# Layer 0 of a streaming encoder step: prompt rows turned as loaded, first loads and first projections in another order

## What is computed

```
h  = rms_norm(x, ln_attn[l])                      # x * 1/sqrt(mean(x*x) + eps) * gain
z  = einsum('btd,de->bte', h, w_in[l])            # 1024 -> 1184 columns
#    columns 0:512 q_a, 512:640 k_a, 640:768 v_a, 768:1024 q latent, 1024:1152 kv latent, 1152:1184 rotary key
#    every part: rms_norm per head, rotary turn of q_a, k_a and the rotary key
o  = concat(sliding-window attention (keys: band or cache), latent attention (keys: own or cached latent))
x  = x + einsum('btm,md->btd', o, w_o[l])
x  = x + (swiglu(rms_norm(x)) if l == 0 else top-2-of-8 experts(rms_norm(x)))
```

## Time and profile before

| | |
|---|---|
| runs | 1201.98, 1202.36, 1204.39 us; median 1202.36 |
| the profiled execution's own time | 1203.37 us |
| its span in the trace | 1201.5 us |
| attention of layer 0 | 0 to 146 us |
| dense layer | 146 to about 380 us |
| attention of layer 1 | to about 500 us |
| experts | about 505 to 1190 us |

### The profile page before, as it was taken

One profiled execution on the slowest core, in us unless ns is written; L12 is line 12 of the kernel. 1 busy time (PEld: TensorE's weight loads), 2 busy tenths in 40 slices (PEclk: granted clock), 3 DMA queues, 4 the chain that ended last, 5 costly groups with the idle time before them and its releaser, 6 DMA issues.

```text
span 1201.5 us, 24345 instructions
## 1 busy us (share of the span) xinstructions
PE 1179.6 (98%) x10285; PEld 618.4 (51%) x10285; DVE 548.7 (46%) x1035; ACT 329.9 (27%) x612; POOL 80.3 (7%) x179
## 2 busy tenths in 40 slices
PE   8999999999999999999999999999999999999998
PEld 5566699999995566533333333333333333333254
DVE  2677534544414667533433434354264244334334
ACT  2576533443324556310210210210200200211101
POOL 4132000000001120000000000000000100100100
PEclk9999999999999999999999999999999999999999
DMA  9261294554530353999999999999999999999996
GB/s 304 60 168 37 92 285 150 174 175 132 162 125 1 63 132 125 352 369 375 406 389 413 398 399 413 399 398 414 399 396 415 399 399 415 390 408 414 392 410 256
DMA packets 114104, 348.56 MB, mean 290 GB/s; under 512 B 8592, under 2 KB 34032, under 8 KB 103808
## 3 DMA queue, kind: packets, MB, share of 16 engines
q1 hardware_dynamic: 108656, 335.55, 74.4%
q0 software_dynamic: 3648, 10.60, 3.1%
q10 hardware_dynamic: 1744, 1.61, 0.4%
HBM read 339.70 MB, written 8.04 MB: 289 GB/s over the span
## 4 chain that ended last, share of the span: by engine, by line
PE 86%; DMA 6%; DVE 4%; ACT 2%; SPq 1%; issue 1%; DVEq 0%; ACTq 0%
PE ps L2439 34%; PE ps L2446 17%; PE ps L2344 12%; PE ps L2075 8%; PE ps L2360 6%; DMA ring<-in_moe_w_gate 2%; DMA ring<-in_moe_w_down 2%; DMA ring<-in_w_in 2%; SPq L736 1%; PE ps L2274 1%; PE ps L2221 1%; PE ps L2236 1%; PE ps L2166 1%; PE ps L2155 1%; PE ps L2088 1%
## 5 line engine op out<-in xcount | busy, mean ns | idle before, releaser
L2439 PE MATMUL ps<-ring,xg 128*32 128x512 f32 (+1 forms) x1792 | 197.6, 547 | 1.2 <-DMA ring<-in_moe_w_gate 0.8
L1857 DVE STREAM_TRANSPOSE am<-act_m 32x256 f32<-32x256 f32 (+1 forms) x288 | 172.6, 599 | 4.7
L2439 PE MATMUL ps<-ring_more,xg 128*32 128x512 f32 (+1 forms) x1280 | 149.7, 571 | 0.0
L1351 DVE TENSOR_TENSOR w_lo<-ring,w_hi 128x2048 fp32r<-128x2048 f32 (+1 forms) x34 | 76.0, 2234 | 96.2 <-ACT w_hi L941 96.2
L2075 PE MATMUL ps<-ring,hT 128*128 128x512 f32 x256 | 115.4, 596 | 0.1
L2439 PEld LDWEIGHTS ps<-ring,xg 128*32 128x32 f32 x1792 | 58.0, 110 | 111.2 <-issue 106.4
L1842 DVE TENSOR_TENSOR act_m<-act_m,ps 64x512 f32<-64x512 f32 (+1 forms) x24 | 15.2, 635 | 213.1 <-ACT act_m L1290 213.1
L2439 PE MATMUL ps<-ring_more,am 128*32 128x512 f32 x896 | 108.9, 592 | 0.0
L2446 PE MATMUL ps<-ring,xg 128*32 128x512 f32 (+1 forms) x896 | 106.7, 547 | 0.0
L2344 PE MATMUL ps<-hT_hi,w_hi 128*128 128x288 f32 x352 | 104.3, 296 | 0.5 <-DVE hT_lo L1725 0.5
L2344 PE MATMUL ps<-hT_lo,w_hi 128*128 128x288 f32 x352 | 103.8, 295 | 0.0
(11 more groups left out here) (388 smaller groups left out, 1539.2 us busy)
## 6 DMA issues: line engine op xcount, KB each, us to landing
ring_more<-in_moe_w_down SPq DMA_DIRECT2D x64, 1024.0 KB, 16.0
ring<-in_moe_w_gate SPq DMA_DIRECT2D x48, 1024.0 KB, 17.0
ring_more<-in_moe_w_up SPq DMA_DIRECT2D x48, 1024.0 KB, 16.2
ring<-in_moe_w_gate SPq DMA_DIRECT2D x32, 768.0 KB, 18.6
ring_more<-in_moe_w_gate SPq DMA_DIRECT2D x16, 1024.0 KB, 14.7
ring<-in_moe_w_up SPq DMA_DIRECT2D x16, 1024.0 KB, 18.4
ring<-in_moe_w_down SPq DMA_DIRECT2D x16, 1024.0 KB, 15.5
ring<-in_moe_w_up SPq DMA_DIRECT2D x16, 768.0 KB, 14.7
```

Source lines behind the costliest of these rows:

```text
L1351: V.tensor_tensor(lo[:, 0:size], src[:, 0:size], hi[:, 0:size].bitcast(F32), ALU.subtract).then_inc(lo_ready, 1)
L1857: ins = V.transpose(am[GRAN * q:GRAN * q + GRAN, c % 2, 0:nk, GRAN * g:GRAN * g + GRAN], src)
L2439: ins = mm_(ps[GRAN * s_:GRAN * s_ + GRAN, b, 0:half], x[:, GRAN * g:GRAN * g + GRAN], w[:, half * h:half * h + half], start=(n == 0), sto ...
```

## The change

Prompt tiles of layer 0 are turned as they were loaded, without the scaling on VectorE, and their scale is applied when the projections are taken out, as in layer 1. TensorE turns tile 0 first, then the gains' rows, the decode tile, and tile 1 only after the first half block of tile 0. The decode projection comes behind three half blocks of tile 0 instead of two, and `za` 0,1,1 and `za` 1,0,1 are each one step of their kind earlier. Of seven filler matmuls in front of the `h` steps two stay. SyncE loads prompt tile 1 ahead of the third quarter of the weights, and the constants ahead of the fourth. GpSimd loads the router and layer 1's caches after the last row step of layer 0, and the caches have a semaphore for each layer.

```diff
-PE_ORDER = [[("h", 2), ("h", 0), ("h", 1), ("za", 0, 0, 0), ("za", 0, 0, 1), ("tc",), ("za", 2), ("zc", 0), ("za", 0, 1, 0),
-             ("item", 0), ("za", 1, 0, 0), ("tq", 2), ("za", 0, 1, 1), ("titem", 0), ("item", 1), ("s", 0), ("item", 2),
-             ("za", 1, 0, 1), ("za", 1, 1, 0), ("p", 0), ("za", 1, 1, 1), ("titem", 1), ("o", 0), ("tq", 0), ("zc", 1),
+PE_ORDER = [[("h", 0), ("ln",), ("h", 2), ("za", 0, 0, 0), ("h", 1), ("za", 0, 0, 1), ("za", 0, 1, 0), ("tc",), ("za", 2), ("zc", 0),
+             ("item", 0), ("za", 0, 1, 1), ("za", 1, 0, 0), ("tq", 2), ("za", 1, 0, 1), ("titem", 0), ("item", 1), ("s", 0), ("item", 2),
+             ("za", 1, 1, 0), ("p", 0), ("za", 1, 1, 1), ("titem", 1), ("o", 0), ("tq", 0), ("zc", 1),
...
-              ("isq", 0), ("ir", 0), ("tqe", 2), ("zev", 0, 1), ("tie", 0), ("isq", 1), ("zr", 0), ("e", 0), ("ir", 1),
+              ("isq", 0), ("ir", 0), ("zev", 0, 1), ("tqe", 2), ("tie", 0), ("isq", 1), ("zr", 0), ("e", 0), ("ir", 1),
...
-DVE_ORDER = [[("x1", 2), ("ln",), ("x1", 0), ("hd", 2), ("x1", 1), ("hd", 0), ("hd", 1), ("z1", 2), ("z2", 2), ("i1", 0),
+DVE_ORDER = [[("x1", 2), ("ln",), ("r1", 0), ("hd", 0), ("hd", 2), ("r1", 1), ("hd", 1), ("z1", 2), ("z2", 2), ("i1", 0),
...
-WAITING = [{("h", 2): 4, ("h", 0): 2, ("h", 1): 1, ("p", 1): 1, ("o", 1): 4, ("s", 3): 1, ("p", 2): 3, ("o", 2): 2, ("hf", 1): 6},
+WAITING = [{("h", 2): 2, ("p", 1): 1, ("o", 1): 4, ("s", 3): 1, ("p", 2): 3, ("o", 2): 2, ("hf", 1): 6},
...
-            for t in TILES:
+            def load_rows(t):
+
                 src = a["x_sample"][0] if t == 2 else a["x_prompt"][0, t * P:(t + 1) * P, :]
                 sp.dma_start(xres[0:ROWS[t], t, :], src).then_inc(loaded_x[t], 16)
+
+            load_rows(2)
+            load_rows(0)
...
                 if key == ("in", 0, 1, 0):
+                    load_rows(1)
+                elif key == ("in", 0, 1, 1):
                     sp.dma_start(cst[:, P:CONST_W], consts[:, P:CONST_W]).then_inc(loaded_c, 16)
...
-            pool.dma_start(wr[:, :, :], a["moe_router"][0].rearrange("(k p) e -> p k e", p=P)).then_inc(loaded_cache, 16)
-            for l in range(DEPTH):
+            def load_caches(l):
...
+            load_caches(0)
...
                 pool.wait_ge(rows_ready, 3 * l + 3)
+                if l == 0:
+                    pool.dma_start(wr[:, :, :], a["moe_router"][0].rearrange("(k p) e -> p k e", p=P)).then_inc(loaded_router, 16)
+                    load_caches(1)
...
-                        by = 1.0 if l == 0 else rsx[:, t:t + 1]
-                        if l:
-                            act.wait_ge(scale_x, t + 1)
+                        by = rsx[:, t:t + 1]
+                        act.wait_ge(scale_x, 2 * l + t + 1)
...
-            pe.wait_ge(loaded_ln, 32)
             ident = C("ident")
-            tr(ps[:, 0, 0:4 * KD], ln_rows[0:4 * KD, :], ident[0:4 * KD, 0:4 * KD]).then_inc(ln_done, 1)
...
+                    if kind == "ln":
+
+                        pe.wait_ge(loaded_ln, 32)
+                        tr(ps[:, 0, 0:4 * KD], ln_rows[0:4 * KD, :], ident[0:4 * KD, 0:4 * KD]).then_inc(ln_done, 1)
...
-                    elif kind == "h" and l == 1 and which[0] < 2:
+                    elif kind == "h" and which[0] < 2:
...
-                        wait_out(pe, ("tz", KD - 3))
+                        if l:
+                            wait_out(pe, ("tz", KD - 3))
+                        else:
+                            pe.wait_ge(loaded_x[t], 16)
...
-                        pe.wait_ge(loaded_cache, CACHES_IN)
+                        pe.wait_ge(loaded_cache[l], CACHES_IN)
```

More of the change, by code:

```diff
@@ L426, in build @@
         loaded_g = [sem(f"loaded_g{l}") for l in range(DEPTH)]
-        loaded_cache = sem("loaded_cache")
+        loaded_cache = [sem(f"loaded_cache{l}") for l in range(DEPTH)]
+        loaded_router = sem("loaded_router")
         loaded_col = sem("loaded_col")
@@ L659, in build @@
         GAINS_IN = 16 * len(GAIN)
-        CACHES_IN = 16 * (1 + 4 * DEPTH)
+        CACHES_IN = 16 * 4
         block = ctx.enter_context(nc.Block())
@@ L776, in _ @@
         def _(pool):
-            pool.dma_start(wr[:, :, :], a["moe_router"][0].rearrange("(k p) e -> p k e", p=P)).then_inc(loaded_cache, 16)
-            for l in range(DEPTH):
-                pool.dma_start(kc[:, l, :], a["cache_swa_k"][l, 0].rearrange("s h d -> s (h d)")).then_inc(loaded_cache, 16)
-                pool.dma_start(vc[:, l, :], a["cache_swa_v"][l, 0].rearrange("s h d -> s (h d)")).then_inc(loaded_cache, 16)
-                pool.dma_start(ckvc[:, l, :], a["cache_mla_ckv"][l, 0]).then_inc(loaded_cache, 16)
-                pool.dma_start(krc[:, l, :], a["cache_mla_krope"][l, 0]).then_inc(loaded_cache, 16)
+            def load_caches(l):
+                pool.dma_start(kc[:, l, :], a["cache_swa_k"][l, 0].rearrange("s h d -> s (h d)")).then_inc(loaded_cache[l], 16)
+                pool.dma_start(vc[:, l, :], a["cache_swa_v"][l, 0].rearrange("s h d -> s (h d)")).then_inc(loaded_cache[l], 16)
+                pool.dma_start(ckvc[:, l, :], a["cache_mla_ckv"][l, 0]).then_inc(loaded_cache[l], 16)
+                pool.dma_start(krc[:, l, :], a["cache_mla_krope"][l, 0]).then_inc(loaded_cache[l], 16)
+            load_caches(0)
             for l in range(DEPTH):
@@ L841, in rope_part @@
                     if t == 2:
-                        pool.wait_ge(loaded_cache, CACHES_IN)
+                        pool.wait_ge(loaded_cache[l], CACHES_IN)
                     own = krc[:, l, :] if t == 2 else kr[0:r, min(t, 2), :]
@@ L1437, in expert_tables @@
                 dve.wait_ge(tables_clear, 1)
+                dve.wait_ge(loaded_router, 16)
                 V.tensor_tensor(wr[:, :, :], wr[:, :, :], bc(ln_cols[:, 3 * KD:4 * KD], NE), ALU.mult).then_inc(router_scaled, 1)
@@ L1975, in _ @@
                         busy(ps[:, 0, :], WAITING[l][step])
-                    if kind == "hf" and l == 1:
+                    if kind == "ln":
+                        pe.wait_ge(loaded_ln, 32)
+                        tr(ps[:, 0, 0:4 * KD], ln_rows[0:4 * KD, :], ident[0:4 * KD, 0:4 * KD]).then_inc(ln_done, 1)
+                    elif kind == "hf" and l == 1:
                         t, = which
@@ L2003, in _ @@
                         busy(pair(key), WAITING[l].get(step, 0))
-                        wait_out(pe, ("tz", KD - 3))
+                        if l:
+                            wait_out(pe, ("tz", KD - 3))
+                        else:
+                            pe.wait_ge(loaded_x[t], 16)
                         for k in range(KD):
-                            if k == 4:
+                            if l and k == 4:
                                 wait_out(pe, ("tz", KD - 1))
```

## The result

The changed kernel takes 1208.09 us (median of 7 runs, 1206.34 to 1209.52); the kernel before, run beside it, 1203.06 (7 runs, 1201.98 to 1204.41). The ratio is 1.0037, 95% interval 1.0028 to 1.0046. So it is slower, by 3.4 to 5.5 us with that interval; the forecast was 1199.4 with a range up to 1202.2.

The account below looks back on a forecast made before the run. TensorE was taken as the bound, with the first weights' transfers on the chain early. Terms -3.43 moved block, +0.13 later start, 0 tables, +0.3 behind made -3.0: 1202.36 to 1199.4 us, range 1197.5 to 1202.2.

Parts of the forecast that it names:

- One projection step moves into the wait: Layer 0 prelude: `za` 0,1,0 runs before the fourth weight quarter lands, taking 3.43 us out of what follows.
- Less ahead in the queues: Prelude loads: with 240 KB fewer and a new order, first quarter at 9.9, tile 1's rows 14.4, fourth quarter 25.8.
- Is TensorE in time?: Prelude: three blocks done by 24.4, no wait for the fourth quarter, `zc` 0 ends at 31.5; gain 3.3 us.
- rival 3: `za` 0,0,0 to `za` 0,1,0: clock stays low, each block costs 3.43 us more; +5, 1207 us; chance 0.07.
- Tables: GpSimd's tables after the gain loads: gains land at 29.2, tables end at 34.3, just out of the way; cost 0.
- Rival 1: Gains land at 31 or later, TensorE stands at `tq` 2 for 1 to 2.5 us: 1201.2; chance 0.25.
- What comes after 34.80 is released by events of the kernel ... so what is won by then is won at the end: After the prelude: time won by 34.80 reaches the end of the kernel unless a wait eats it.
- the rest of the attention: Layer 0 attention behind the prelude: slower evacuations, VectorE timing and fewer blocks before `p` 0 cost 0.3 us together.
- Rival 2: Layer 0 attention: ScalarE and VectorE set its end, gain becomes waits before `titem` 1 and 2; 1202 to 1202.6; chance 0.08.
- Five of seven filler matmuls go; by themselves they cover nothing: Prelude, before the `h` steps: removing five fillers was given no cost of its own in the sum.
- dense layer and experts as long as before: Everything behind layer 0's attention: durations unchanged, listed as a sign that the forecast was right.
- The rule I weighed: Prelude: dropped fillers and a stand at tile 1's rows risk the lower clock; by it alone, some us worse.

Follow-up runs that it names:

- the second profile of the changed kernel: The changed kernel, unaltered, run once more beside later versions: 1207.66 us, ratio 1.0036.
- item 1 early: `i2` 1 ahead of tile 0's `z2` on VectorE, item 1's root earlier on ScalarE: changed kernel with five fillers back 1200.48 us; kernel before 1203.47.
- the kernel with the order alone: Kernel before with item 1 early and `za` 0,1,0 ahead of the cached keys' turning and decode projection, loads as before: 1206.74 us.
- the fillers late: Changed kernel with five filler matmuls added in layer 1's attention (`o` of group 2) instead of the prelude: 1205.79 us, ratio 1.0023.
- the fastest version with three fewer: Changed kernel with five fillers back, item 1 early and keys' up-projection loaded before queries', then three prelude fillers taken out: 1204.13 us.

## Why the prediction was wrong

*One projection step moves into the wait* was right: TensorE reached the end of `zc` 0 at 31.0 (31.5 forecast).

*Less ahead in the queues* was right but for one transfer: first quarter 9.9 (9.9; the exact hit is luck, three more profiles with the same prelude have 10.1 to 10.7), tile 1's rows 14.0 (14.4). I named `b_w_ukv` among the loads and gave it no landing time. It came at 31.9, and `item` 0 waited 0.95 us (0.47 in the second profile of the changed kernel).

*Is TensorE in time?* was right: three blocks done at 24.1 (24.4), eight records on the lower level in 6.55 us, full clock from 16.3. So rival 3 (clock stays low) fell.

*Tables*: gains landed at 27.0 (29.2) and the tables ended at 32.8 (34.3), 1.6 us before `z2` took them; `z2` was released by ScalarE's root. Rival 1 fell.

*"What comes after 34.80 is released by events of the kernel ... so what is won by then is won at the end"* failed, with its term of 0.3 for *the rest of the attention*. `item` 0 was 2.7 us early, and at `p` 0 TensorE stood 2.96 us. My own text had the reason: "Between `s` 0 and `p` 0 stands one block now instead of two". I weighed that against the decode exponentials only, which end "with little room", and didn't look for what else `p` 0 waits on: the pair that `i2` 1 empties, 8 us behind the start of `s` 0 in both kernels, and half a microsecond ahead of `p` 0 in the kernel before. With a block less in that stretch TensorE has 5.2 us of work for those 8. "TensorE arrives 3 us earlier at items 1 and 2" was wrong too: `item` 1 starts at 45.79, before at 44.99, since a third half block now stands in front of it. Rival 2 was this in kind (chance 0.08); it named other places (`titem` 1 and 2) and I argued it away by the hand-over at 64.76, which shows who is last there and not who waits earlier. The runs show it: with item 1 early 3.2 us come back in the changed order, and in the kernel before nothing does.

*"Five of seven filler matmuls go; by themselves they cover nothing"* and *dense layer and experts as long as before* failed. They cover nothing indeed, but they are length. The loss, 3.16 us of standing and 1.7 us at the lower clock less 1.3 us of waits that went, is most of the difference between 1208 and 1203, and no rival held it. The rows before show no stand, so I couldn't have known the sign; that the program's length changes in front of a loop's exit I could have listed as a cost bounded by nothing.

The rule I weighed, that idle stretches send the clock back, would have been of use at another place than I looked. The trace agrees behind the loop: 3.16 us without work, then 0.50. Ahead of `p` 0 it doesn't: 2.96 us without work, then 1.00 in the same kernel.

On code, the Trainium skill, "Runtime: NRT & Kernel Launch" (Instruction fetch mechanics), says that instructions come in blocks of 16 KiB, prefetched strictly in sequence, and that a taken branch to outside what is held costs a fetch. The block size agrees with the profile page of the changed kernel (0.67 MB in 41 packets, 16 KB each; the page of the kernel before has the same line):

```profile
q8 instruction: 41, 0.67, 0.2%
```

The stand seen here is not at a branch taken but behind the exit of a loop, where the next block in sequence is asked for only at the exit (its packet starts 1.4 to 1.7 us later); it lasts 2.3 to 3.8 us by where the cut lies.

## What to carry to other kernels

Before crediting a gain on one engine, find the next place where it meets another engine's chain and measure the room there; moving work of the bound engine out of a wait wins only what the other chains can follow. Work moved from behind a step to in front of it delays what the step starts and leaves less to cover it: count both. When instructions are added to or taken from the busiest engine of a program with a hardware loop, look first at the instructions right behind the loop's exit in the new profile: an idle time released by "issue" there can be code arriving late, which the packets of the instruction queue in the loop's first turn show, and a few harmless instructions anywhere in front move it away. Filler instructions have three effects to be told apart (cover a wait, hold the clock, shift the code), and it takes one run each: drop them, and put them elsewhere.

## What was unexpected in the hardware

- Leaving a loop can cost a fetch: the code behind a fixed cut arrives 4.0 to 4.2 us after the exit, in six profiles of five kernels. Eight records more in front of the cut shortened the stand by 0.86 us by arithmetic and 0.86 (3.16 to 2.30) by measurement.
- A loop of some 600 us was held whole: its code packets came in its first turn, and between 600 and 1100 us none of the fourteen profiles has one.
- Idle time of TensorE of about the same length was followed by the lower clock level at one place and mostly not at another. Behind the loop 2.3 to 3.8 us of it were, in five profiles of six; the price was 1.7 us in the changed kernel. The 3.15 us of the kernel with the order alone were too. Ahead of `p` 0 2.96 or 2.97 us were in one of five. At the start of the experts 0.7 us of standing were in two of fourteen (0.50 and 0.66 in 506 to 510 with the fillers late; 0.54 and 0.61 in 502 to 506 in the fastest version with three fewer), and each cost 1.7 us. What decides it, no run here shows.
- The start of the dense layer varies by 1.5 us between profiled executions of near-identical preludes (144.74 to 146.22), because the first weights land at different times. A gain of a microsecond read from one pair of profiles in such a prelude is not a result.
